# Turns, additions, scaling and row writes of a routing stage in another order

## The chip, the cores and the metric

The kernel runs on one core of one Trainium2 chip. The metric is device time in microseconds (us), median of three runs. Inputs and results are float32.

## The reference, cut to what matters

Two transformer blocks on 512 tokens of width 1024. The change lies in the first one, between the output projection of its second attention (`w_mo`) and its mixture of experts:

```
x = x + (memory attention output) @ w_mo            # 512 x 1024
h = rms_norm(x, norm_moe_w)
g = h @ w_group      (4 groups);  e = h @ w_router  (4 x 8 experts)
grp = argmax(g); top 2 experts of that group
gates = softmax(g)[grp] * softmax(top two logits)
for each expert: y = (silu(xb @ w_gate) * (xb @ w_up)) @ w_down   # xb = its rows of h
x = x + sum of gate * y
```

Every expert's three matrices of 2 MB are read: 32 x 3 x 2 MB.

## The kernel before, in words

Each engine has its own hand-written program, and the engines meet in counted semaphores: `X.tick(key)` raises one, `wait_ge(*X.at(key))` waits for it. An engine works strictly in the order in which its code was written.

The tokens are four tiles of 128 rows, i = 0 to 3. `w_mo` is two panels of 512 columns. `projecting` (L498) multiplies a panel in eight steps (half of the contraction, tile) of 12 matmuls of 128x512. The last panel uses the order `BY_TILE` (L494): (0,0) (0,1) (1,0) (1,1) (0,2) (1,2) (0,3) (1,3); I number these steps 0 to 7. A tile of the panel is done at its step with half 1: tile 0 after step 2, tile 1 after step 3, tile 2 after step 5, tile 3 after step 7. `behind[n]` is called after step n, `after(i)` when tile i is done.

`dve_router` (L1744) first splits the two weight units of the last panel (`dve_cut`, L451, behind `act_cut`, L440, on ScalarE; the second of them needs the buffer that panel 0 reads until its last matmul), then adds panel 0 to X (four `dve_add`, L1334), then handles the last panel tile by tile: add, mean of squares (ScalarE squares, L581; GpSimd takes the root, L591), copy of the turned features from PSUM, and `dve_scale` (L597), which writes the normed rows that go to memory as `scratch_h`.

`flip` turns (transposes) the 1024 columns of a tile of X in two halves of four 128x128 blocks: half 0 needs only panel 0's result, half 1 the last panel's. VectorE copies half 0 to SBUF, ScalarE half 1 (L1736). `logit(i)` multiplies tile i's turned features with the 36 router columns (8 float32 matmuls, recorded as 16). Before, flip(i) stands one tile late in the last panel and logit(i) two tiles late; flip(3), logit(2), logit(3) stand behind it.

PSUM has eight banks. `Banks.take` (L119) goes round among the banks of a set and makes TensorE wait until the last user of the bank has let it go. Followed through the code, panel 0 of `w_mo` has banks 0, 1, 2, 3 for tiles 0 to 3 and the last panel 4, 5, 0, 1. The turns use the set `LOGITS` = banks 2, 3, 7 in this order, the first of them bank 2, which is let go by the addition of panel 0's tile 2.

Behind the logits VectorE chooses the experts, TensorE counts how many tokens of each expert stand ahead (`count`), VectorE makes places of it, TensorE and VectorE turn these to lists of rows (`places`, `dve_rows`, L1828). GpSimd's program (`pool_router`, L1852, then L2106) waits until all four tiles of rows are written to `scratch_h` and the lists are there, and gathers the rows of the first expert pair by an indirect DMA. VectorE cleans the gathered rows (`dve_clean`, L1847: rows that stand for no token become zero), TensorE turns them, and the first product (L1962) starts. The gates (L1817 to L1824) stand behind this cleaning and are used behind the first product.

SyncE's queue: `sp_load` (L1923) loads one expert matrix (2 MB) to one of nine slots; loads 0 to 8 need no earlier load's slot. From load 9 on, a load waits until the product that read its slot's last content is done; loads 9 to 12 go in two parts, the first waits until half of the product is done. Before, loads 5 and 6 stand behind the end of the last panel and behind the row writes of tiles 0 to 2, load 7 behind that of tile 3, load 8 behind the landing of the first gather.

Of the kernel before, what the change touches and what calls it, by code (L numbers as in the profile page):

```python
# [13 lines left out]
ACT = mybir.ActivationFunctionType  # L14
# [5 lines left out]
NT = 4  # L20
# [419 lines left out]
def act_cut(k, u, part=None):  # L440

    w = k.w
    at = half_of(part, w.units[u][0] * w.units[u][1])
    k.A.wait_ge(*w.landed[u % RAW].at(u))
    if w.prior[u] is not None:
        k.A.wait_ge(*w.freed[w.prior[u]])
    k.A.e.activation(w.splits[w.split_of[u]][0][:, at], w.rows(u)[:, at], ACT.Copy).then_inc(  # L447
        *(w.half_hi if part == 0 else w.hi).tick(u))
# [30 lines left out]
def flips(k, bank, srcs):  # L479
    for n, s in enumerate(srcs):  # L480
        m = s.shape[0]
        ins = k.T.e.transpose(bank[0:s.shape[1], 128 * n:128 * n + m], s, k.ident[0:m, 0:m])  # L482
    return ins


def blocks_of(rows, n=8):
    return [rows[:, 128 * c:128 * c + 128] for c in range(n)]
# [50 lines left out]
def finish(steps):  # L538
    for _ in steps:
        pass  # L540
# [44 lines left out]
def dve_mean(k, site, i):  # L585
    ss = k.rstat[site, i]
    k.V.wait_ge(*k.squared.at(site, i))
    k.V.e.tensor_scalar(ss, ss, 1.0 / D, 1e-6, ALU.mult, ALU.add).then_inc(*k.meant.tick(site, i))
# [8 lines left out]
def dve_scale(k, site, i, src, rows, gain):  # L597
    k.V.wait_ge(*k.rooted.at(site, i))
    k.V.e.scalar_tensor_tensor(out=rows, in0=src, scalar=k.rstat[site, i], in1=gain, op0=ALU.mult,
                               op1=ALU.mult).then_inc(*k.rowed.tick(site, i))  # L600
# [733 lines left out]
def dve_add(k, name, half, i, scale):  # L1334

    V, ve = k.V, k.V.e
    xs, bank = k.X[:, i, 512 * half:512 * half + 512], k.banks[name, half, i]
    V.wait_ge(*k.projected.at(name, half, i))
    if scale is None:
        ins = ve.tensor_tensor(xs, xs, bank[:], ALU.add)  # L1340
    else:
        ins = ve.scalar_tensor_tensor(out=xs, in0=xs, scalar=scale, in1=bank[:], op0=ALU.mult, op1=ALU.add)
    ins.then_inc(*k.res.tick(name, half, i))
    V.wait_ge(*k.res.at(name, half, i))
# [104 lines left out]
def mem_out(k, half, **kw):  # L1449
    return projecting(k, "w_mo", half, k.start["w_mo"] + 2 * half, NT,  # L1450
                      lambda i: [k.mix_lo.at("mem", i, 0), k.mix_lo.at("mem", i, 1)],
                      lambda i: k.res.at("w_mo", half, i), **kw)
# [220 lines left out]
def pe_router(k):  # L1673
    T, te, u0 = k.T, k.T.e, k.start["w_mo"]
    logits = k.banks.take(T, ("logits",), k.dve_step.at("router", "logits"), hold=True, of=Banks.FLIPS)

    def flip(i):
        T.wait_ge(*k.res.at("w_mo", 1, i))
        for half in range(2):
            bank = k.banks.take(T, ("moe", i, half), (k.h_odd if half else k.h_even).at(i), of=Banks.LOGITS)  # L1680
            flips(k, bank, blocks_of(k.X[:, i, :])[4 * half:4 * half + 4]).then_inc(*k.h_turned.tick(i, half))

    def logit(i):
        T.wait_ge(*k.dve_step.at("router", "gain"))
        T.wait_ge(*k.h_even.at(i))
        T.wait_ge(*k.h_odd.at(i))
        group(te, logits[:, 36 * i:36 * i + 36],
              [(k.xn[:, c, 128 * i:128 * i + 128], k.rw[:, c, :]) for c in range(KT)]).then_inc(*k.pe_step.tick("router", i))

    def behind(i):  # L1690
        if i:
            flip(i - 1)
        if i > 1:
            logit(i - 2)
    finish(mem_out(k, 1, after=behind, steps=BY_TILE))
    flip(3)
    logit(2)
    logit(3)
    k.banks.release(("logits",))
    bank = k.banks.take(T, ("count",), k.dve_step.at("places", "marked"))  # L1700
    T.wait_ge(*k.dve_step.at("router", "chosen"))
    ones, strict = k.tri[:, 511:639], k.tri[:, 383:511]
    te.matmul(bank[:, 0:128], strict, k.ms, start=True, stop=True, skip_group_check=True)
    for c in (3, 2, 1):
        ins = te.matmul(bank[:, 128 - 32 * c:128], ones, k.ms[:, 0:c, :], start=False, stop=True, skip_group_check=True)
    ins.then_inc(*k.pe_step.tick("count"))
    bank = k.banks.take(T, ("total",), k.dve_step.at("router", "count"))
    ins = group(te, bank[:, 0:32], [(ones, k.ms[:, i, :]) for i in range(NT)])
    ins.then_inc(*k.pe_step.tick("total"))
    pe_places(k, "places", 0, NPAIR, k.pe_step, k.dve_step)  # L1710
# [15 lines left out]
def act_router(k):  # L1726
    A, ae, u0 = k.A, k.A.e, k.start["w_mo"]
    act_cut(k, u0 + 2)
    act_cut(k, u0 + 3)
    for i in range(NT):  # L1730
        A.wait_ge(*k.res.at("w_mo", 1, i))
        if i == 3:
            A.wait_ge(*k.hd_out[0].at())
        act_square(k, "moe", i, k.X[:, i, :], k.xg[i % 3])
        A.wait_ge(*k.h_turned.at(i, 1))
        ae.activation(k.xn[:, 4:8, 128 * i:128 * i + 128], k.banks["moe", i, 1][:].rearrange("p (k t) -> p k t", k=4),  # L1736
                      ACT.Copy).then_inc(*k.h_odd.tick(i))
    A.wait_ge(*k.dve_step.at("router", "less"))
    ae.activation(k.s44, k.s44, ACT.Exp).then_inc(*k.act_step.tick("router", "group"))
    A.wait_ge(*k.dve_step.at("router", "apart"))  # L1740
    ae.activation(k.dr[:, 0:4], k.dr[:, 0:4], ACT.Exp).then_inc(*k.act_step.tick("router", "pair"))


def dve_router(k):  # L1744
    V, ve, u0 = k.V, k.V.e, k.start["w_mo"]
# [6 lines left out]
    ve.tensor_tensor(k.rw, k.rw, k.gainT.unsqueeze(2).to_broadcast([P, 8, 36]), ALU.mult).then_inc(  # L1752
        *k.dve_step.tick("router", "gain"))
    V.wait_ge(*k.om_in[1].at("moe"))
    for i in range(NT):
        dve_add(k, "w_mo", 1, i, None)
        dve_mean(k, "moe", i)
        V.wait_ge(*k.h_turned.at(i, 0))
        ve.tensor_copy(k.xn[:, 0:4, 128 * i:128 * i + 128],
                       k.banks["moe", i, 0][:].rearrange("p (k t) -> p k t", k=4)).then_inc(*k.h_even.tick(i))  # L1760
        dve_scale(k, "moe", i, k.X[:, i, :], k.xg[i % 3], k.om[1][:])
    V.wait_ge(*k.pe_step.at("router", 3))
    b3 = k.banks["logits",][:, 0:144].rearrange("p (i n) -> p i n", i=4)
    rstd = k.rstd.unsqueeze(2)
# [32 lines left out]
    ve.tensor_tensor(dr[:, 0:4], k.em[:, :, 1], k.em[:, :, 0], ALU.subtract).then_inc(*k.dve_step.tick("router", "apart"))  # L1797
    m01 = k.m01.rearrange("p c i n -> p (c i) n")
    ve.tensor_tensor(k.token1[:, :, 0, :], m01, k.tokv.unsqueeze(2).to_broadcast([P, 8, 32]), ALU.mult)
    V.wait_ge(*k.pe_step.at("count"))  # L1800
    pos = k.banks["count",][:, 0:128].rearrange("p (i n) -> p i n", i=4)
    for c in range(2):
# [4 lines left out]
                     k.pk.unsqueeze(2).to_broadcast([P, 8, 64]), ALU.is_equal).then_inc(*k.dve_step.tick("places", "marked"))  # L1807
    V.wait_ge(*k.pe_step.at("places"))
    dve_rows(k, "places", NPAIR, k.dve_step)
    dve_clean(k, k.x1, 0)  # L1810
    V.wait_ge(*k.pe_step.at("total"))
    ve.tensor_copy(k.cnt, k.banks["total",][:, 0:32]).then_inc(*k.dve_step.tick("router", "count"))
    V.wait_ge(*k.dve_step.at("router", "count"))
# [9 lines left out]
    V.settle(ve.tensor_tensor(gate[:, 1, :], gate[:, 0, :], dr[:, 0:4], ALU.mult))  # L1823
    ve.tensor_tensor(k.token1[:, :, 1, :], m01, gate.rearrange("p c i -> p (c i)").unsqueeze(2).to_broadcast([P, 8, 32]),  # L1824
                     ALU.mult).then_inc(*k.dve_step.tick("gates", "marked"))


def dve_rows(k, what, n, dve_step):  # L1828
# [18 lines left out]
def dve_clean(k, x, n):  # L1847
    k.V.wait_ge(*x.gathered[n % 3].at(n))
    k.V.e.tensor_scalar(k.xg[n % 3], k.xg[n % 3], k.taken[:, n:n + 1], None, ALU.mult).then_inc(*x.cleaned.tick(n))
# [9 lines left out]
def sp_router(k):  # L1859
    Y, a, x, mo = k.Y, k.a, k.x1, k.start["w_mo"]  # L1860
    Y.wait_ge(*k.w.freed[mo - 1])
    sp_load(k, x, 0)
    Y.wait_ge(*k.w.lo.at(mo + 1))
    sp_load(k, x, 1)
    Y.wait_ge(*k.applied.at("mem", 15))
    Y.e.dma_start(k.rw[:, :, 0:4], a["w_group"][0].rearrange("(k p) n -> p k n", p=P)).then_inc(*k.c3_in.tick(0))
    for g in range(4):
        Y.e.dma_start(k.rw[:, :, 4 + 8 * g:12 + 8 * g],
                      a["w_router"][0, g].rearrange("(k p) n -> p k n", p=P)).then_inc(*k.c3_in.tick(1 + g))
    for n, (dst, src) in enumerate(((k.tri, a["c_tri"]), (k.iota, a["c_iota"]), (k.tokv, a["c_tok"]),  # L1870
                                    (k.gainT, a["l_moe"]), (k.cap, a["c_cap"]))):
        Y.e.dma_start(dst, src).then_inc(*k.c3_in.tick(5 + n))
    sp_load(k, x, 2)
    sp_load(k, x, 3)
    Y.wait_ge(*k.w.lo.at(mo + 3))
    sp_load(k, x, 4)
    for i in range(NT):
        if i == 3:
            Y.wait_ge(*k.projected.at("w_mo", 1, 3))
            sp_load(k, x, 5)  # L1880
            sp_load(k, x, 6)
        Y.wait_ge(*k.rowed.at("moe", i))
        Y.e.dma_start(k.hd[128 * i:128 * i + 128, :], k.xg[i % 3]).then_inc(*k.hd_out[i].tick())
    sp_load(k, x, 7)
    Y.wait_ge(*x.gathered[0].at(0))
    sp_load(k, x, 8)

# [1559 lines left out]
```

## Time and profile before

| | |
|---|---|
| median of three runs | 2345.57 us (2345.16 to 2345.81) |
| the profiled execution's own time | 2346.38 us |
| its span | 2345.1 us |
| TensorE busy | 2227.9 us, 95% |
| VectorE busy | 1020.5 us, 44% |
| ScalarE busy | 716.6 us, 31% |
| DMA | 370.27 MB, mean 158 GB/s |
| chain that ended last | TensorE 76%, DMA 9%, VectorE 6%, issue 5%, ScalarE 3% |

The busy shares are means over stages. The expert stage (about 510 to 990 us) has DMAs busy in all slices and the rest of the kernel does not, so the stage and not the mean tells what bounds it. PE is TensorE's matmuls, DVE VectorE, ACT ScalarE, POOL GpSimd, SPq SyncE's DMA issues.

### The profile page before, as it was taken

Reading aid. Unit: us, or ns where it says so; the run is one execution under the profiler, and the core shown is the slowest. Engines: PE = TensorE matmul, PEld = TensorE weight load, DVE = VectorE, ACT = ScalarE, POOL = GpSimd, SP = SyncE. Lnnn points to the kernel's source line nnn. Section 1 sums busy time; section 2 is a strip of 40 time slices with the busy share of each in tenths; the row PEclk is TensorE's granted clock in tenths of the full one; section 3 lists DMA queues with packets and bytes.
Section 4 is the critical chain, followed back from the end, with each engine's and each line's share of the span. In section 5 each row is a group of like instructions: output and inputs, shape, how many; then the busy total and the mean of one; then the engine's idle time right before and its main releaser. Section 6 shows DMA issues by size and latency. Waiting matters only on the chain.

```text
span 2345.1 us, 28330 instructions
## 1 busy us (share of the span) xinstructions
PE 2227.9 (95%) x11771; PEld 1642.0 (70%) x11771; DVE 1020.5 (44%) x1860; ACT 716.6 (31%) x1251; POOL 104.3 (4%) x109
## 2 busy tenths in 40 slices
PE   8998999979999899899879999999999999999998
PEld 7866787754433334488656788888878778888887
DVE  5356464332322222533567643233532456433334
ACT  5335354210100000222456233133233462331330
POOL 2001001010000000000000000000000001000001
PEclk9999999979999999999989999999999999999999
DMA  5233341369999999722110333222142202322320
GB/s 203 90 126 99 111 167 67 124 242 421 427 426 427 427 426 428 280 92 77 45 43 1 101 116 108 90 94 104 38 156 90 72 2 69 112 90 93 105 90 36
DMA packets 107316, 370.27 MB, mean 158 GB/s; under 512 B 15232, under 2 KB 20736, under 8 KB 94384
## 3 DMA queue, kind: packets, MB, share of 16 engines
q1 hardware_dynamic: 104160, 361.58, 40.6%
q0 software_dynamic: 3024, 6.83, 0.9%
q8 instruction: 95, 1.56, 0.3%
q14 instruction: 37, 0.30, 0.0%
HBM read 368.32 MB, written 4.19 MB: 159 GB/s over the span
## 4 chain that ended last, share of the span: by engine, by line
PE 76%; DMA 9%; DVE 6%; issue 5%; ACT 3%; POOL 1%; SPq 0%; DVEq 0%; ACTq 0%; POOLq 0%
PE PB L465 51%; PE PB L1962 10%; PE PB L482 4%; PE PB L784 4%; DMA FL_raw<-in_w_exp_gate 3%; PE PB L475 3%; PE PB L676 2%; DMA Z<-in_w_exp_gate 1%; DMA FH_raw<-in_w_exp_gate 1%; DMA W_raw<-in_w_exp_down 1%; PE PB L800 1%; DMA FL_raw<-in_w_exp_down 1%; PE PB L681 1%; ACT nsp L710 1%; DMA scratch_h<-Z 1%
## 5 line engine op out<-in xcount | busy, mean ns | idle before, releaser
L465 PE MATMUL PB<-W,FH 128*128 128x512 f32 (+1 forms) x1792 | 555.0, 392 | 8.0 <-DVE FL L845 4.0
L456 DVE TENSOR_TENSOR W<-R,W 128x2048 fp32r<-128x2048 f32 (+2 forms) x130 | 291.6, 2244 | 598.7 <-ACT W L447 598.7
L447 ACT ACTIVATE W<-R 128x2048 fp32r<-128x2048 f32 (+2 forms) x130 | 243.8, 1876 | 639.9 <-PE PB L465 636.2
L465 PEld LDWEIGHTS PB<-W,FH 128*128 128x128 f32 x1792 | 330.0, 189 | 76.0 <-issue 5.4
L465 PE MATMUL PB<-W,hid 128*128 128x512 f32 x1536 | 349.4, 390 | 0.0
L465 PE MATMUL PB<-W,FL 128*128 128x512 f32 (+1 forms) x896 | 347.5, 388 | 0.0
L465 PEld LDWEIGHTS PB<-W,hid 128*128 128x128 f32 x1536 | 288.3, 188 | 59.6
L465 PE MATMUL PB<-FH,W 128*128 128x512 f32 (+1 forms) x1152 | 324.2, 366 | 1.3 <-DVE FL L570 1.3
L465 PEld LDWEIGHTS PB<-FH,W 128*128 128x128 f32 x1152 | 208.5, 189 | 37.2 <-issue 1.8
L465 PE MATMUL PB<-FL,W 128*128 128x512 f32 (+1 forms) x576 | 210.7, 366 | 0.0
L465 PEld LDWEIGHTS PB<-W,FL 128*128 128x128 f32 x896 | 168.7, 188 | 34.5
L1962 PE MATMUL PB<-R,om 128*64 128x512 f32 x320 | 150.1, 625 | 15.2 <-DMA Z<-in_w_exp_gate 7.6
L1962 PE MATMUL PB<-Z,om 128*64 128x512 f32 x304 | 126.0, 616 | 0.8 <-issue 0.8
L465 PEld LDWEIGHTS PB<-FL,W 128*128 128x128 f32 x576 | 108.7, 189 | 17.5
L482 PEld LDWEIGHTS PB<-ident,nsp 128*128 128x128 f32 x674 | 80.1, 148 | 42.0 <-issue 27.2
L482 PE MATMUL PB<-ident,nsp 128*128 128x128 f32 x674 | 103.2, 282 | 5.3 <-ACT nsp L710 2.2
L710 ACT ACTIVATE nsp<-nsp,stat 128x512 f32<-128x512 f32 (+3 forms) x146 | 83.3, 572 | 74.9 <-DVE stat L692 74.5
L2037 ACT ACTIVATE tmp_r<-PB 128x512 fp32r<-128x512 f32 x32 | 17.4, 594 | 261.0 <-PE PB L1962 261.0
L676 PE MATMUL PB<-Z 64*128 64x512 f32 (+4 forms) x416 | 94.4, 517 | 2.7 <-ACT om L2735 1.8
L784 PE MATMUL PB<-ptr,Z 128*64 128x128 f32 (+1 forms) x768 | 78.9, 282 | 17.5 <-ACT ptr L734 10.8
L692 DVE CUSTOM_DVE_ANT_0 nsp<-PB,Z 128x512 f32<-128x512 f32 (+3 forms) x146 | 69.0, 510 | 53.0 <-PE PB L676 38.6
L1962 PEld LDWEIGHTS PB<-R,om 128*64 128x64 f32 x320 | 44.6, 144 | 65.2 <-issue 65.2
(340 smaller groups left out, 2576.5 us busy)
## 6 DMA issues: line engine op xcount, KB each, us to landing
R<-in_mlp_w_up SPq DMA_DIRECT2D x32, 1024.0 KB, 5.3
R<-in_mlp_w_down SPq DMA_DIRECT2D x32, 1024.0 KB, 4.9
Z<-in_w_exp_down SPq DMA_DIRECT2D x13, 2048.0 KB, 29.1
Z<-in_w_exp_up SPq DMA_DIRECT2D x12, 2048.0 KB, 34.2
R<-in_w_exp_gate SPq DMA_DIRECT2D x10, 2048.0 KB, 33.3
W_raw<-in_w_exp_up SPq DMA_DIRECT2D x10, 2048.0 KB, 31.3
R<-in_w_exp_up SPq DMA_DIRECT2D x9, 2048.0 KB, 30.9
R<-in_w_in SPq DMA_DIRECT2D x12, 1024.0 KB, 5.5
```

Source lines behind the costliest of these rows:

```text
L447: k.A.e.activation(w.splits[w.split_of[u]][0][:, at], w.rows(u)[:, at], ACT.Copy).then_inc(*(w.half_hi if part == 0 else w.hi).tick(u))
L456: k.V.e.tensor_tensor(wl[:, at], w.rows(u)[:, at], wh[:, at].bitcast(F32), ALU.subtract).then_inc(*(w.half_lo if part == 0 else w.lo).tick(u))
L465: ins = te.matmul(bank, l, r, start=(start and n == 0), stop=(stop and n == len(terms) - 1), skip_group_check=True)
L475: ins = te.matmul(bank, l, r, start=(n == 0), stop=(n == len(pairs) - 1))
L482: ins = k.T.e.transpose(bank[0:s.shape[1], 128 * n:128 * n + m], s, k.ident[0:m, 0:m])
L676: ins = k.T.e.matmul(bank[:, 0:t.n], t.q, t.keys, start=True, stop=(t.more is None))
L681: k.T.e.matmul(bank[:, 0:t.n], *t.more, start=False, stop=True).then_inc(*k.scored.tick(*t.key))
L692: V.e.tensor_tensor_reduce(ns[:, 0:t.n], k.banks[("scores",) + t.key][:, 0:t.n], t.tab, 1.0, FAR, ALU.add, ALU.min, peak(k, m)).then_inc(* ...
L710: k.A.e.activation(ns[:, 0:t.n], ns[:, 0:t.n], ACT.Exp, bias=peak(k, m), scale=-1.0, accum_out=t.den).then_inc(*k.exped.tick(*t.key))
L784: ins = T.e.matmul(k.banks["sums", *t.bank[0]][t.rows, at], l, r, start=first, stop=last, skip_group_check=True)
L800: ins = T.e.matmul(bank[rows, 128 * c:128 * c + 128], col, k.ident[:], start=True, stop=True, skip_group_check=True)
L1962: ins = T.e.matmul(bank[64 * side:64 * side + 64, :], lhs[:, 128 * c + 64 * side:128 * c + 64 * side + 64], ws[side][:, c, at], start=(c = ...
```

## The change

Five edits. (1) Turns are made by halves and earlier: behind step 0 turn (tile 0, half 0), behind step 1 (1,0), step 3 (0,1), step 4 (1,1) and (2,0), step 5 logit(0), step 6 (2,1), (3,0) and logit(1); behind the panel logit(2), turn (3,1), logit(3). VectorE copies tile 3's second half too, which ScalarE did. (2) VectorE's order is written out: the last tile's addition stands ahead of its mean and its copy, with the earlier tiles' scaling moved between. (3) The scaling of tile 3 stands behind the choice, ahead of the wait for `count`. (4) The row writes move from SyncE's to ScalarE's queue; that of tile 3 stands behind both exponentials. Loads 5, 6 and 7 stand directly behind the end of the last panel. (5) The gates stand ahead of the first cleaning.

```diff
--- before.py
+++ after.py
@@ -1674,11 +1674,10 @@
     T, te, u0 = k.T, k.T.e, k.start["w_mo"]
     logits = k.banks.take(T, ("logits",), k.dve_step.at("router", "logits"), hold=True, of=Banks.FLIPS)
 
-    def flip(i):
-        T.wait_ge(*k.res.at("w_mo", 1, i))
-        for half in range(2):
-            bank = k.banks.take(T, ("moe", i, half), (k.h_odd if half else k.h_even).at(i), of=Banks.LOGITS)
-            flips(k, bank, blocks_of(k.X[:, i, :])[4 * half:4 * half + 4]).then_inc(*k.h_turned.tick(i, half))
+    def flip(i, half):
+        T.wait_ge(*k.res.at("w_mo", half, i))
+        bank = k.banks.take(T, ("moe", i, half), (k.h_odd if half else k.h_even).at(i), of=Banks.LOGITS)
+        flips(k, bank, blocks_of(k.X[:, i, :])[4 * half:4 * half + 4]).then_inc(*k.h_turned.tick(i, half))
 
     def logit(i):
         T.wait_ge(*k.dve_step.at("router", "gain"))
@@ -1687,14 +1686,18 @@
         group(te, logits[:, 36 * i:36 * i + 36],
               [(k.xn[:, c, 128 * i:128 * i + 128], k.rw[:, c, :]) for c in range(KT)]).then_inc(*k.pe_step.tick("router", i))
 
-    def behind(i):
-        if i:
-            flip(i - 1)
-        if i > 1:
-            logit(i - 2)
-    finish(mem_out(k, 1, after=behind, steps=BY_TILE))
-    flip(3)
+    def middle():
+        flip(1, 1)
+        flip(2, 0)
+
+    def late():
+        flip(2, 1)
+        flip(3, 0)
+        logit(1)
+    finish(mem_out(k, 1, steps=BY_TILE, behind={0: lambda: flip(0, 0), 1: lambda: flip(1, 0), 3: lambda: flip(0, 1),
+                                                4: middle, 5: lambda: logit(0), 6: late}))
     logit(2)
+    flip(3, 1)
     logit(3)
     k.banks.release(("logits",))
     bank = k.banks.take(T, ("count",), k.dve_step.at("places", "marked"))
@@ -1727,18 +1730,27 @@
     A, ae, u0 = k.A, k.A.e, k.start["w_mo"]
     act_cut(k, u0 + 2)
     act_cut(k, u0 + 3)
+
+    def store(i):
+        A.wait_ge(*k.rowed.at("moe", i))
+        ae.dma_start(k.hd[128 * i:128 * i + 128, :], k.xg[i % 3]).then_inc(*k.hd_out[i].tick())
     for i in range(NT):
         A.wait_ge(*k.res.at("w_mo", 1, i))
         if i == 3:
+            store(2)
             A.wait_ge(*k.hd_out[0].at())
         act_square(k, "moe", i, k.X[:, i, :], k.xg[i % 3])
-        A.wait_ge(*k.h_turned.at(i, 1))
-        ae.activation(k.xn[:, 4:8, 128 * i:128 * i + 128], k.banks["moe", i, 1][:].rearrange("p (k t) -> p k t", k=4),
-                      ACT.Copy).then_inc(*k.h_odd.tick(i))
+        if i < 3:
+            A.wait_ge(*k.h_turned.at(i, 1))
+            ae.activation(k.xn[:, 4:8, 128 * i:128 * i + 128], k.banks["moe", i, 1][:].rearrange("p (k t) -> p k t", k=4),
+                          ACT.Copy).then_inc(*k.h_odd.tick(i))
+        if i in (1, 2):
+            store(i - 1)
     A.wait_ge(*k.dve_step.at("router", "less"))
     ae.activation(k.s44, k.s44, ACT.Exp).then_inc(*k.act_step.tick("router", "group"))
     A.wait_ge(*k.dve_step.at("router", "apart"))
     ae.activation(k.dr[:, 0:4], k.dr[:, 0:4], ACT.Exp).then_inc(*k.act_step.tick("router", "pair"))
+    store(3)
 
 
 def dve_router(k):
@@ -1752,13 +1764,32 @@
     ve.tensor_tensor(k.rw, k.rw, k.gainT.unsqueeze(2).to_broadcast([P, 8, 36]), ALU.mult).then_inc(
         *k.dve_step.tick("router", "gain"))
     V.wait_ge(*k.om_in[1].at("moe"))
-    for i in range(NT):
-        dve_add(k, "w_mo", 1, i, None)
-        dve_mean(k, "moe", i)
-        V.wait_ge(*k.h_turned.at(i, 0))
-        ve.tensor_copy(k.xn[:, 0:4, 128 * i:128 * i + 128],
-                       k.banks["moe", i, 0][:].rearrange("p (k t) -> p k t", k=4)).then_inc(*k.h_even.tick(i))
+
+    def features(i, half):
+        V.wait_ge(*k.h_turned.at(i, half))
+        ve.tensor_copy(k.xn[:, 4 * half:4 * half + 4, 128 * i:128 * i + 128],
+                       k.banks["moe", i, half][:].rearrange("p (k t) -> p k t", k=4)).then_inc(
+            *(k.h_odd if half else k.h_even).tick(i))
+
+    def scale(i):
         dve_scale(k, "moe", i, k.X[:, i, :], k.xg[i % 3], k.om[1][:])
+    features(0, 0)
+    features(1, 0)
+    dve_add(k, "w_mo", 1, 0, None)
+    dve_mean(k, "moe", 0)
+    dve_add(k, "w_mo", 1, 1, None)
+    scale(0)
+    dve_mean(k, "moe", 1)
+    scale(1)
+    features(2, 0)
+    dve_add(k, "w_mo", 1, 2, None)
+    dve_mean(k, "moe", 2)
+    features(3, 0)
+    scale(2)
+    dve_add(k, "w_mo", 1, 3, None)
+    features(3, 1)
+    dve_mean(k, "moe", 3)
+    V.wait_ge(*k.rooted.at("moe", 3))
     V.wait_ge(*k.pe_step.at("router", 3))
     b3 = k.banks["logits",][:, 0:144].rearrange("p (i n) -> p i n", i=4)
     rstd = k.rstd.unsqueeze(2)
@@ -1797,6 +1828,7 @@
     ve.tensor_tensor(dr[:, 0:4], k.em[:, :, 1], k.em[:, :, 0], ALU.subtract).then_inc(*k.dve_step.tick("router", "apart"))
     m01 = k.m01.rearrange("p c i n -> p (c i) n")
     ve.tensor_tensor(k.token1[:, :, 0, :], m01, k.tokv.unsqueeze(2).to_broadcast([P, 8, 32]), ALU.mult)
+    scale(3)
     V.wait_ge(*k.pe_step.at("count"))
     pos = k.banks["count",][:, 0:128].rearrange("p (i n) -> p i n", i=4)
     for c in range(2):
@@ -1807,7 +1839,6 @@
                      k.pk.unsqueeze(2).to_broadcast([P, 8, 64]), ALU.is_equal).then_inc(*k.dve_step.tick("places", "marked"))
     V.wait_ge(*k.pe_step.at("places"))
     dve_rows(k, "places", NPAIR, k.dve_step)
-    dve_clean(k, k.x1, 0)
     V.wait_ge(*k.pe_step.at("total"))
     ve.tensor_copy(k.cnt, k.banks["total",][:, 0:32]).then_inc(*k.dve_step.tick("router", "count"))
     V.wait_ge(*k.dve_step.at("router", "count"))
@@ -1823,6 +1854,7 @@
     V.settle(ve.tensor_tensor(gate[:, 1, :], gate[:, 0, :], dr[:, 0:4], ALU.mult))
     ve.tensor_tensor(k.token1[:, :, 1, :], m01, gate.rearrange("p c i -> p (c i)").unsqueeze(2).to_broadcast([P, 8, 32]),
                      ALU.mult).then_inc(*k.dve_step.tick("gates", "marked"))
+    dve_clean(k, k.x1, 0)
 
 
 def dve_rows(k, what, n, dve_step):
@@ -1874,14 +1906,9 @@
     sp_load(k, x, 3)
     Y.wait_ge(*k.w.lo.at(mo + 3))
     sp_load(k, x, 4)
-    for i in range(NT):
-        if i == 3:
-            Y.wait_ge(*k.projected.at("w_mo", 1, 3))
-            sp_load(k, x, 5)
-            sp_load(k, x, 6)
-        Y.wait_ge(*k.rowed.at("moe", i))
-        Y.e.dma_start(k.hd[128 * i:128 * i + 128, :], k.xg[i % 3]).then_inc(*k.hd_out[i].tick())
-    sp_load(k, x, 7)
+    Y.wait_ge(*k.projected.at("w_mo", 1, 3))
+    for u in range(5, 8):
+        sp_load(k, x, u)
     Y.wait_ge(*x.gathered[0].at(0))
     sp_load(k, x, 8)
```

## Rows read from the trace of the kernel before

**Rows 1.** The page's 40 slices: DMA share in tenths.

```profile
DMA  5233341369999999722110333222142202322320
```

**Rows 2.** Stretches of the span: busy times, then granted clock, DMA share, GB/s.

```profile
522.00:523.00 1.00, 1.00 (x6) 0.35 (x4) 0.00 (x0) 0.00 (x0) 0.00 (x0) 0.64 0.08 33
...
524.35:600.00 75.65, 74.59 (x390) 31.87 (x387) 21.26 (x34) 8.10 (x15) 3.96 (x4) 1.00 1.00 416
...
900.00:956.00 56.00, 50.47 (x236) 21.66 (x232) 16.28 (x26) 4.84 (x9) 0.16 (x1) 1.00 1.01 428
```

**Rows 3.** The chain that ended last, 474 to 956 us: start, duration, what.

```profile
474.69 5.47 PE PB L465 x24
480.17 0.87 PE PB L482 x8
481.04 1.71 PE PB L475 x16
...
494.67 13.76 DMA scratch_h<-Z
...
509.45 4.47 DMA Z<-scratch_h,Z
...
515.17 1.97 PE PB L482 x8
...
517.97 9.42 PE PB L1962 x32
...
933.79 22.15 DMA FL_raw<-in_w_exp_down
```

**Rows 4.** VectorE in order of time, 467 to 518 us: start, duration, line, what.

```profile
467.19 2.85 DVE L1340 TENSOR_TENSOR X<-X,PB 128x512 f32<-128x512 f32 x4
...
488.77 0.69 DVE L1759 COPY FH_raw<-PB 128x512 f32<-128x512 f32 x1 [4.20 <-PE PB L482]
...
493.35 1.29 DVE L599 SCALAR_TENSOR_TENSOR Z<-X,stat,om 128x1024 f32<-128x1024 f32 x1
496.26 0.17 DVE L1765 TENSOR_TENSOR Z<-PB,stat 128x16 f32<-128x16 f32 x1 [1.62 <-PE PB L475]
...
501.31 0.42 DVE L1799 TENSOR_TENSOR nsp<-Z 128x256 f32<-128x256 f32 x1
503.25 0.49 DVE L1803 TENSOR_TENSOR tmp<-PB,Z 128x128 f32<-128x128 f32 x2 [1.51 <-PE PB L1705]
...
507.12 0.17 DVE L1834 TENSOR_TENSOR Z<-tmp,Z 128x16 uint32<-128x16 f32 x1
...
516.76 0.43 DVE L1824 TENSOR_TENSOR nsp<-Z 128x256 f32<-128x256 f32 x1
```

**Rows 5.** ScalarE, TensorE and SyncE's queue in order of time.

```profile
463.03 1.92 ACT L447 ACTIVATE W<-R 128x2048 fp32r<-128x2048 f32 x1 [3.52 <-PE PB L465]
...
491.30 1.09 PE L482 MATMUL PB<-ident,X 128*128 128x128 f32 x8 [0.43 <-DVE X L1340]
...
491.04 0.43 SPq L1940 DMA_DIRECT2D FL_raw<-in_w_exp_gate  x1
...
523.97 0.33 SPq L1940 DMA_DIRECT2D Z<-in_w_exp_down  x1
```

**Rows 6.** Stretches with a falling or rising granted clock, columns as in Rows 2.

```profile
495.00:496.00 1.00, 1.00 (x8) 1.00 (x7) 0.00 (x0) 0.00 (x0) 0.00 (x0) 0.70 0.87 360
...
663.00:664.00 1.00, 0.76 (x4) 0.00 (x0) 0.00 (x0) 0.17 (x1) 0.00 (x0) 1.00 1.04 442
...
666.00:667.00 1.00, 0.39 (x2) 0.32 (x4) 1.00 (x2) 0.00 (x0) 0.00 (x0) 0.54 1.00 426
...
669.00:670.00 1.00, 1.00 (x6) 0.42 (x4) 0.00 (x0) 0.00 (x0) 0.00 (x0) 0.76 0.92 393
```

**Rows 7.** DMA issues, whole span: count, KB each, median us from issue to landing.

```profile
scratch_h<-Z SPq DMA_DIRECT2D x4, 512.0 KB, 2.8
Z<-scratch_h,Z POOLq DMA_INDIRECT x16, 10.4
```

## The prediction

> **What bounds the kernel now.** I read first the page's slices [rows 1]: the DMAs are busy without a gap from the tenth slice to the sixteenth, while the kernel as a whole uses 158 GB/s. Then the stretches of that part [rows 2]: from 524 us on the 16 DMA engines have share 1.00 and 416 GB/s, at the end 1.01 and 428 GB/s; just before, at 522 to 523, the share is 0.08. The chain [rows 3] ends its weight stage on such a transfer (started 933.79, landed 955.94) and not on arithmetic. So from load 9 on, issued at 523.97 [rows 5], when half of the first expert product is done, the stage is a fixed quantity of bytes: loads 9 to 95 are 87 x 2.097 MB = 182.5 MB, which in 432 us (523.97 to 955.94) is 422 GB/s, with the gathers 427 to 428. Nothing behind 524 can be made up or lost there: **each us by which the first product starts earlier or later goes to the end one to one.** The question is thus what the change does to the 60 us ahead of it.
>
> There the chain runs, in order [rows 3]: the last panel with its turns and logits, tile 3's row write (issued 494.67, landed 13.76 us later, at 508.43), the first gather (from 509.45, 4.47 us), cleaning and turning, the first product at 517.97. Beside it runs a second chain, VectorE's [rows 4]: logits at 496.26, choice, places, the lists of rows ready at 507.29 (507.12 plus 0.17). It is 1.1 us shorter than the row write's. A change has to shorten both to win more than 1.1 us, and lengthening the second by more than 1.1 us already costs.
>
> **Edit 1, the turns.** The turn behind step 0 waits for two things: panel 0's addition of tile 0, and bank 2, which that panel's tile 2 holds. VectorE makes the four additions from 467.19 in 2.85 us [rows 4], 0.71 each, so the third ends at 469.3. They can't come earlier: they stand behind VectorE's cut, that needs ScalarE's (463.03 to 464.95), and that waited for TensorE to end panel 0 [rows 5]. TensorE itself: steps 4 and 5 begin at 474.69 behind the turn of tile 0 (0.87), so step 3 ends at 473.82; a step takes 5.47 / 2 = 2.735 us [rows 3], so step 0 began at 473.82 - 4 x 2.735 = 462.9 and ends at 465.6. Before, no turn was due until 473.8 and no wait showed. After, TensorE stands in its order at a turn that can't start: 469.35 - 465.6 = **+3.7 us** on the engine that both chains need. Nothing hides it: steps 1 to 7 are queued behind.
>
> *Clock.* Idle TensorE of this length is not in this stretch of the trace. The nearest: idle from 663.76, back at 666.6; the granted clock fell to half at about 666.1 (mean 0.54) and was back at 669.5 (mean 0.76) [rows 6], 3.4 us at half. Work in half clock loses half its time, so bounds are 0 and 1.7 us. If it falls 2.3 us into the idle time and stays 3.4, it lasts to 471.3 and meets 2.0 us of work: **+1.0**.
>
> *Tail.* The work is the same in number: eight steps, eight half turns of 0.435 (0.87 per pair), four logits of 1.71 [rows 3]. The idle 0.43 ahead of turn 3 [rows 5] goes, since logit(2) now covers the addition: **-0.4**. But turn (3,1), its copy and logit(3) now follow each other with nothing between: 0.69 for the copy [rows 4], some 0.2 for two hand-overs and the end of the turn: **+0.9** (bounds 0.7 and 1.2). At 495 to 496 the clock was falling (0.70) [rows 6]; from 495.4 to 496.2 the last logit ran at half. With the dense steps ending later it is likely spared: **-0.4** (to 0). Other turns wait for nothing: their halves and banks are free by over 1 us in the order written out. Sum to the logits: 3.7 + 1.0 - 0.4 + 0.9 - 0.4 = **+4.8** (3.8 to 6.2): 501.1 in place of 496.26.
>
> **Edits 2 and 3, VectorE.** The last addition still follows step 7 directly; mean, root and scalings lie under TensorE's work. The scaling of tile 3, 1.29 us, comes behind the instruction at 501.31 and ahead of the one at 503.25, which waits 1.51 us for `count` [rows 4]: 501.7 to 502.95, 0 us. Without that cover (a `count` at full clock, some 0.9 us shorter) it would cost what `count` gains. So the lists come at 507.29 + 4.8 = **512.1** (511.1 to 513.5).
>
> **Edit 4, the row writes.** Tile 3's rows were ready at 494.64; now behind the choice: 501.73 + 4.8 + 1.29 = 507.8, issued at 508.0. The three weight loads used to be issued from 491.04 [rows 5] among the row writes; now at the end of step 7: 462.9 + 8 x 2.735 + 7 x 0.435 + 2 x 1.71 + 4.7 = 495.9. Their 6.29 MB take 14.7 us at 427 GB/s and 1 us to start, to 511.7. Where the row write lands beside them is not in the trace. Alone it takes 2.8 (the median of four, three on a quiet DMA) [rows 7]: 510.8. Behind everything: 511.7 + 2.8 = 514.5. Nearest row: gathers, from GpSimd's queue, land in a median of 10.4 us [rows 7] beside queued loads, and in 4.47 on quiet DMAs [rows 3], so a second queue gets a small share while loads are queued. I take 513.0. For tiles 0 to 2 nothing changes.
>
> In sentences that the sum does without: the Trainium skill (DMA: Bandwidth & Descriptors, section Queues, rings and completion order) says that every DMA engine goes round between the queues that have work, a packet at a time; by it the write would take half the bandwidth at once and land at about 511.9, before the lists. The same page (Issuing engines are not separate DMA queues) says that another issuing engine saves only the time to issue, which would put it near 513.5. The gathers' 10.4 us lean to the second.
>
> GpSimd then wakes at max(512.1, 513.0) = 513.0 in place of 508.43: **+4.6** (2.7 to 7.1). Its 1.0 us to the gather and the gather's 4.47 stay.
>
> **Edit 5, gates.** They ended at 517.19 [rows 4], 0.05 behind the turns of the first rows (515.17 plus 1.97 us [rows 3]), whose copy waited on both: less than 0.1 us is won. In their new place they lie between the lists and the landing, 5 us with VectorE idle: 0.
>
> **First product.** Its first 4.7 us ran at half clock (517.97 to 522.7, mean 0.64 at 522 to 523) [rows 2], 2.4 us lost. Where the clock comes back after a start that is later by another amount, no row says; bounds 0 and -2.4; nearest is its own row, so **-0.3**.
>
> Sum: 4.6 - 0.3 = +4.3. Against the profiled execution's 2346.38 that is 2350.7; that execution lies 0.8 above the median of the runs, so for the median 2345.57 + 4.3 = **2349.9 us**, +0.18%. I count 0.2% (4.7 us) as what can be told from no change, so this is "same", close to the edge. Its own range is 2347.6 to 2351.0.
>
> **Rivals.**
> *A, the row write waits out the loads.* Place: tile 3's write on ScalarE's queue. Landing at 514.5, with a clock loss nearer 1.7 at 515.1: GpSimd wakes 6.1 to 6.7 later, the end is 5.8 to 6.4 later: 2351.6, slower. It decides from a landing behind 513.1. For it: the same write took 13.76 us among loads before; the 10.4 of the gathers. Against it: only some 3 us of load are left when it starts.
> *B, the lists decide.* The write shares evenly with the loads (the skill's first rule above) and lands before 512.1: 512.1 - 508.43 = 3.7, less 0.3: 2349.0. For it: 0.5 MB is little; against it: the gathers.
> *C, the change does what it says.* TensorE is not held at the turn of step 0, because the additions or the bank come earlier than I read. Then the choice is at 496.3 or 0.1 to 0.4 later, lists at 507.5, row write covered: -1.0, with up to 2.4 from the clock: 2344.5 (2342.2 to 2345). For it: the tail wait of 0.43 goes, the write's 13.76 us leave the chain. Against it: the cut and the additions keep their order in the code and end at 469.3 in the trace.
>
> **How the numbers follow.** Forecast 0.42, A 0.36, B 0.13, C 0.09. "Same" takes six sevenths of the forecast, B, and about two thirds of C: 0.36 + 0.13 + 0.06 = 0.55. Slower is A and the rest of the forecast: 0.42 less a part in which A's landing is met by an early clock: 0.40. Faster 0.05, from C at its low end and what I don't see. The range leaves out the lowest part of C and the upper tail of A (every bound at its worst is +6.8): 2346.6 to 2352.2.
>
> **What would show it.** TensorE idle of 3.7 us from 465.6, ended by VectorE's additions; a stretch at half clock behind it; the last logit at about 501; the lists at 512; tile 3's write issued at 508; the gather at 514; load 9 at about 528; the stage's DMA share 1.0 to about 960. No idle at 465 makes step 1 wrong; a landing before the lists makes B right; an end of the weight stage that moves less than load 9 makes the one to one wrong.

## The result, and the profile of the changed kernel

The changed kernel takes 2353.01 us (median of 7 runs, 2352.15 to 2356.05) against 2345.57 (7 runs, 2341.34 to 2349.18): ratio 1.0036, 95% interval 1.0027 to 1.0045. It is slower by 7.4 us, more than the 4.3 that I forecast (2349.9), and outside my range (2346.6 to 2352.2).

The profiled execution took 2352.52 us, span 2350.4. First its chain, against [rows 3]:

```profile
470.06 0.70 DVE X L1340
...
470.89 1.08 PE PB L482 x4
471.98 3.60 PE PB L465 x12
...
498.25 1.71 PE PB L475 x16
499.96 0.48 PE PB L482 x4
...
500.54 0.70 DVE FH_raw L1770
...
501.37 1.96 PE PB L475 x16
...
510.13 10.32 DMA scratch_h<-Z
...
521.46 3.54 DMA Z<-scratch_h,Z
...
528.63 8.56 PE PB L1989 x32
```

TensorE waits for VectorE's third addition, makes the half turn of tile 0 in 1.08 us where one takes 0.44, and needs 3.60 for a step of 2.735: the granted clock is at half (1.2 GHz) until 473.6. At the end the copy (L1770) stands alone between a turn and the last logit. Then tile 3's row write takes 10.32 us and the gather follows.

VectorE, against [rows 4], and the idle TensorE ahead of its first turn:

```profile
503.43 0.17 DVE L1796 TENSOR_TENSOR Z<-PB,stat 128x16 f32<-128x16 f32 x1 [2.14 <-PE PB L475]
...
508.48 0.42 DVE L1830 TENSOR_TENSOR nsp<-Z 128x256 f32<-128x256 f32 x1
508.81 1.28 DVE L599 SCALAR_TENSOR_TENSOR Z<-X,stat,om 128x1024 f32<-128x1024 f32 x1
510.41 0.49 DVE L1835 TENSOR_TENSOR tmp<-PB,Z 128x128 f32<-128x128 f32 x2 [0.32 <-PE PB L1708]
...
514.29 0.17 DVE L1866 TENSOR_TENSOR Z<-tmp,Z 128x16 uint32<-128x16 f32 x1
```

```profile
470.89 1.08 PE L482 MATMUL PB<-ident,X 128*128 128x128 f32 x4 [3.81 <-DVE X L1340]
...
501.37 1.95 PE L475 MATMUL PB<-tmp,FH_raw 128*128 128x36 f32 x16 [0.94 <-DVE FH_raw L1770]
```

The scaling (L599) lies in the wait for `count`, of which 0.32 us is left: it is free, as forecast. The lists are ready at 514.46.

All times of this execution are 1.44 us late from its first weight cut on (9.18 us for 7.74, a wait for a DMA), long before the change, so I count from the end of panel 0, which each trace shows by ScalarE's second cut ([rows 5]: 463.03, less 0.14 us; in the changed kernel 464.47). In that count:

| us from the end of panel 0 | before | changed | moved |
|---|---|---|---|
| loads 5 to 7 from | 28.15 | 33.96 | +5.8 |
| logits on VectorE | 33.37 | 39.10 | +5.7 |
| lists ready | 44.40 | 50.13 | +5.7 |
| tile 3's write issued | 31.78 | 45.80 | +14.0 |
| it lands | 45.54 | 56.11 | +10.6 |
| first gather issued | 46.56 | 57.13 | +10.6 |
| load 9 issued | 61.08 | 69.45 | +8.4 |
| next stage's first weight cut on ScalarE | 505.46 | 515.54 | +10.1 |

The span is only 5.3 us longer though the stage lost 10. Matched by ScalarE's instructions, the two executions are 11.5 us apart (1.44 of it from the start) at 968 us of the one before, 8.7 at 1130 and 5.4 at 1201. In between the granted clock differs: of the stretches at half clock that begin between 960 and 1230 us the execution before has six and this one four. That is this pair of executions; the runs of one kernel spread over up to 12 us, and the medians differ by 7.4.

### The profile page after: what moved, and what is told of

Its sections match the earlier page's. It is cut to its first block, busy times and chain, and to the rows that moved or that the text cites. A ratio compares the mean times of both kernels' runs of the same rounds, so it can differ in the third digit from the quotient of the medians.

```text
span 2350.4 us, 28333 instructions
## 1 busy us (share of the span) xinstructions
PE 2223.9 (95%) x11771; PEld 1638.5 (70%) x11771; DVE 1021.4 (43%) x1861; ACT 716.0 (30%) x1250; POOL 104.2 (4%) x109
## 4 chain that ended last, share of the span: by engine, by line
PE 76%; DMA 9%; DVE 6%; issue 5%; ACT 3%; POOL 1%; SPq 0%; DVEq 0%; ACTq 0%; POOLq 0%
PE PB L465 51%; PE PB L1989 9%; PE PB L482 4%; PE PB L784 4%; DMA Z<-in_w_exp_gate 3%; PE PB L475 3%; DMA FH_raw<-in_w_exp_gate 3%; PE PB L676 2%; DMA Z<-in_w_exp_down 1%; DMA FL_raw<-in_w_exp_gate 1%; PE PB L800 1%; PE PB L681 1%; ACT nsp L710 1%; DMA scratch_h<-Z 0%; DVE X L2286 0%
## 5 line engine op out<-in xcount | busy, mean ns | idle before, releaser
L1989 PEld LDWEIGHTS PB<-R,om 128*64 128x64 f32 x320 | 44.6, 144 | 65.7 <-issue 65.7
```

The source lines that it names most:

```text
L1989: ins = T.e.matmul(bank[64 * side:64 * side + 64, :], lhs[:, 128 * c + 64 * side:128 * c + 64 * side + 64], ws[side][:, c, at], start=(c = ...
```

## The experiments

Times vary with the clock, so I judge by the count from panel 0's end and put the time beside it; a ratio is that to the kernel before. Each count is from one profiled execution. How far it repeats is seen at the logits: 33.1 to 33.5 in the five kernels whose code is the same up to there as before (before, experiments 5, 9, 10 and 11), but 39.0 to 41.1 in the six with the stalled turns (changed, 2, 3, 6, 7 and 8), by the granted clock.

**1. No turn behind steps 0 and 1.**

```diff
-behind={0: lambda: flip(0, 0), 1: lambda: flip(1, 0), 3: ...
+behind={2: first, 3: ...          # first: flip(0, 0), flip(1, 0)
```

> The changed kernel with one edit taken back in part: the turns of tiles 0 and 1, half 0, stand behind step 2 of the last panel and not behind steps 0 and 1. Theory (stall): TensorE doesn't stand idle for 3.8 us ahead of them and the clock doesn't fall behind it, so from the end of panel 0 to the logits it takes 5.3 us less (about 33.7 in place of 39.0), and the end of the last panel, the weight loads 5 to 7, the lists and the row write of tile 3 all come earlier by the same, the first gather and load 9 too: time 5 us below the changed kernel, 2 to 3 above the kernel before. Rival (the row write alone is the loss, and it waits for the loads whatever comes before): the logits come 5 us earlier but the time of the gather is set by a write that takes longer than 10.3 us, time within 1.5 us of the changed kernel.

Logits at 34.80 (4.3 us earlier than changed), load 9 at 64.30 (5.2 earlier); 2348.47 us, ratio to before 1.0010 (0.9999 to 1.0021). The idle time and its clock are gone; the last logit took 2.98 us, mostly at half clock, for 1.96, which is the missing us. The write now took 8.54, 1.8 less. The stall theory holds: 5.2 of the 8.4 us at load 9 go with the idle time, the write behind it moving along and growing shorter.

**2. The write without loads beside it.**

```diff
-    for u in range(5, 8): sp_load(k, x, u)
-    Y.wait_ge(*x.gathered[0].at(0)); sp_load(k, x, 8)
+    sp_load(k, x, 5)
+    Y.wait_ge(*x.gathered[0].at(0))
+    for u in range(6, 9): sp_load(k, x, u)
```

> The changed kernel with weight loads 6 and 7 held back until the first gather has landed, where they stood ahead of the row write of tile 3. Theory (the write waits behind the queued loads): tile 3's rows, issued at the same place, land 2.6 to 3.5 us after issue and not 10.3, the gather starts 6 us earlier relative to the end of panel 0, limited by the lists; load 9 is then issued about 6 us earlier, but 4.2 MB more are still to move behind the gather, 9.8 us of DMA, so the time is 0 to 5 us above the changed kernel. Rival (a write issued by ScalarE is slow by itself): it still takes about 10 us.

Tile 3's write, issued at the same 45.84, landed 2.61 us later and no longer ends the wait: the lists (50.17) do (L1843 is VectorE's instruction right behind them), and the gather is issued at 51.11, 6.0 us earlier than in the changed kernel. Tile 2's write, beside load 5 alone, still took 9.33. The median landing of all four writes is 2.7 us:

```profile
517.01 1.13 POOL L2133 DMA_INDIRECT Z<-scratch_h,Z  x1 [13.48 <-DVE Z L1843]
```

```profile
scratch_h<-Z ACTq DMA_DIRECT2D x4, 512.0 KB, 2.7
```

In the changed kernel the median of the four is 6.5. Time 2356.3 us, ratio 1.0039 (1.0025 to 1.0053): load 9 comes at 64.81, but the bytes held back are then missing (450 us from load 9 to the next stage, elsewhere 444 to 447). ScalarE's queue is not slow by itself; the loads beside it are the cause. This answers the rival.

**3. Scaling and write of tile 3 early.**

```diff
-    V.wait_ge(*k.rooted.at("moe", 3))
+    scale(3)                                  # and not behind token1; store(3) ahead of both Exp
```

> The changed kernel with edit 3 taken back: tile 3 is scaled ahead of the choice and its row write stands ahead of the exponentials, issued about 7.5 us earlier. Theory (the write lands when the loads queued at the end of the panel are through, about 19 to 20 us after these were issued): it lands at most 2 to 3 us earlier than in the changed kernel, still behind the lists or together with them; the logits' evaluation starts up to 1 us later since the scaling of 1.29 us stands ahead of it where it isn't covered; time 1 to 4 us below the changed kernel. Rival (the write takes a fixed 10.3 us from issue): it lands 7.5 us earlier, ahead of the lists, which then decide: 5 us below.

The write was issued at 39.21 and took 13.52 us, landing at 52.73, behind the lists (51.99); load 9 at 66.32; 2351.72 us, ratio 1.0025 (1.0012 to 1.0037). Issued 6.6 us earlier, it lands 3.4 us earlier: not a fixed time from issue. It had tile 2's write ahead of it in its queue, which landed at 46.62. In this execution the last logit ran at half clock, so the logits came at 40.96; the early scaling did not hold them up (VectorE still waited 1.77 us for them).

**4. Edit 4 alone on the kernel before.** All four writes from ScalarE's queue, loads 5 to 7 directly behind the panel.

```diff
+        if i in (1, 2): store(i - 1)          # in act_router; store(2) at i == 3, store(3) behind the loop
-        Y.wait_ge(*k.rowed.at("moe", i)); Y.e.dma_start(k.hd[...], k.xg[i % 3])
```

> The kernel before with edit 4 alone: row writes from ScalarE's queue, that of tile 3 directly behind its scaling, loads 5 to 7 directly behind the end of the last panel. Theory: loads 5 to 7 are issued 2.7 to 6 us earlier than before, so the DMAs are through about 3 us earlier, and tile 3's write, issued at 494.7 as before, lands by then, 505 to 506; the lists at 507.3 decide and the first gather starts about 1 us earlier: time 0 to 1.5 us below the kernel before. Rival (a write from ScalarE's queue gets less than from SyncE's): it lands later than 508.4, time 1 to 4 us above the kernel before.

A miss for my theory: loads from 25.43 on, write issued at 32.15 and 16.84 us long, landing at 48.99, 3.5 us later than before, as the rival had it; load 9 at 62.92, 1.8 later. 2346.51 us, ratio 1.0002 (0.9992 to 1.0012), so the time doesn't show it. Three writes stood in ScalarE's queue beside the loads at once and landed one after the other, at 38.5, 44.6 and 49.0:

```profile
490.97 2.40 ACTq L1733 DMA_DIRECT2D scratch_h<-Z  x2
496.80 0.33 ACTq L1733 DMA_DIRECT2D scratch_h<-Z  x1
```

How queues share the DMAs is seen in the changed kernel's packets: queue, packets, MB, share of 16 engines, for 496 to 520 us and then for 510.1 to 513.8, 513.8 to 517.2 and 517.2 to 520.4:

```profile
q1 hardware_dynamic: 432, 6.29, 65.4%
q10 hardware_dynamic: 288, 1.05, 10.8%
...
q1 hardware_dynamic: 107, 1.49, 95.1%
q10 hardware_dynamic: 11, 0.04, 2.7%
...
q1 hardware_dynamic: 76, 1.05, 74.2%
q10 hardware_dynamic: 89, 0.36, 26.0%
...
q10 hardware_dynamic: 46, 0.12, 9.6%
q1 hardware_dynamic: 7, 0.05, 3.7%
```

q1 is SyncE's queue, q10 ScalarE's. 6.29 MB in 432 packets less 48 of 4 bytes is 16 KB each; two writes (tiles 2 and 3) in 288 less 32 are 4 KB each. Until 513.6, 3.5 us behind its issue, tile 3's write moves nothing; then a 4 KB packet goes about one to one with a 16 KB packet (89 to 76), a quarter of the bytes. The DMAs are through with nearly all at 518; until 520 a trickle runs on at share 0.07 and 0.06, that is one DMA engine of 16. In experiment 5, where no other write is in that queue, the counts for 498.9 to 505 us are cleaner (0.52 MB is a quarter of 2.08, so one 4 KB packet for each of 16 KB):

```profile
q1 hardware_dynamic: 143, 2.08, 79.7%
q10 hardware_dynamic: 142, 0.52, 21.0%
```

The Trainium skill (DMA: Bandwidth & Descriptors, section Queues, rings and completion order) has the turns by packets, and these counts agree with it; that turns are not shares of bandwidth is what I overlooked. What becomes of unequal packets this section does not say; these traces show it.

**5. Only tile 3's write on ScalarE's queue.** The kernel before; tiles 0 to 2 stay with SyncE, loads 5 to 7 together behind them.

```diff
+    A.wait_ge(*k.rowed.at("moe", 3))          # in act_router, ahead of the first Exp
+    ae.dma_start(k.hd[384:512, :], k.xg[0]).then_inc(*k.hd_out[3].tick())
```

> The kernel before with only the row write of tile 3 moved to ScalarE's queue, issued at the same place; tiles 0 to 2 stay in SyncE's queue, so nothing stands ahead of it in its own. Theory (queues take turns by packets, 4 KB of the write against 16 KB of a load; 8 packets a DMA engine, so 8 x 0.73 us plus some 3 us to the first): it lands about 10 us after its issue, at 41 to 43 us from the end of panel 0 in place of 45.5, ahead of the lists (44.4), which then decide: gather 1.1 us earlier than before, time 0 to 2 us below the kernel before. Rival (the write lands only when the loads issued ahead of it are through): as before, 13 to 14 us, no gain.

```profile
scratch_h<-Z ACTq DMA_DIRECT2D x1, 512.0 KB, 10.7
```

Issued at 31.78, landed at 42.5, ahead of the lists (44.23), which decide; gather at 45.17, load 9 at 58.59, 2.5 earlier than before. With three loads ahead in the other queue it took 10.7 us, where behind two loads in SyncE's own queue it had taken 13.76: so a queue of its own gains it 3 us here. 2340.1 us, ratio 0.9979 (0.9969 to 0.9990).

**6. Tile 3's write in SyncE's queue, behind the loads.** The changed kernel with `store(3)` moved behind `sp_load` 7.

> The changed kernel with tile 3's row write in SyncE's queue, behind loads 5 to 7, with its issue where the scaling ends as in the change. Theory (turns by packets): behind the 3 loads it is served last but then at the full rate, so it lands about when the queue is empty, 54 to 55.5 us from the end of panel 0 against 56.1: 0 to 2 us earlier than in the changed kernel. Rival (ScalarE's queue is fast, the loads only slow it a little): it lands later than in the changed kernel.

A miss: 9.43 us, landing at 57.15. In this execution the logits were at 41.03, 1.9 us late, which moves all of it: the half clock behind TensorE's idle time lasted 6.8 us and not 3.4. So the landing is later than in the changed kernel, as the rival said, but for this reason: counted from the loads' issue it is 21.7 us, in the changed kernel 22.15. 2354.87 us, ratio 1.0041 (1.0025 to 1.0057). So at this place either queue gives nearly the same: the write ends with the loads.

**7. Loads 5 to 7 in packets of 8 KB.**

```diff
+        for part in range(2): sp_load(k, x, u, part)
```

> The changed kernel with loads 5, 6 and 7 each issued in two parts, which makes their packets 8 KB in place of 16 KB; bytes and order are the same. Theory (turns by packets): each 4 KB packet of the row write now waits for 8 KB, about 0.3 us, so tile 3's write takes 8 x 0.45 us plus up to 3 us, 6 to 8 us in place of 10.3, and the gather comes 2.5 to 4 us earlier. Rival (bandwidth is shared in halves, or the write waits for all loads ahead): it lands within 1 us of where it did, since the bytes ahead of it are the same.

```profile
512.30 8.12 DMA scratch_h<-Z
```

Landing 2.2 us sooner after issue, 8.12 against 10.32, just outside the 6 to 8 that I expected; the logits of this execution were 2.0 us late too, so the gather gained 0.2 and not 2.5 to 4. Time 2353.24, ratio 1.0033 (1.0022 to 1.0044). By itself the landing proves nothing, since the loads had 0.8 us more of a lead (12.65 us against 11.84). The packets of 516 to 518.5 us say more: 80 against 93, still about one for one, though a load's packet is now 8 KB, and the write gets 31% of the bytes and not a quarter:

```profile
q1 hardware_dynamic: 93, 0.74, 69.6%
q10 hardware_dynamic: 80, 0.33, 31.8%
```

**8. The turns without edits 3 and 4.**

> The changed kernel with edits 3 and 4 taken back: scaling of tile 3 ahead of the choice, row writes and loads 5 to 7 in SyncE's queue as before. What is left is the order of the turns, of VectorE and of the gates. Theory (the turns cost 5.3 to 7 us by TensorE's idle time and clock, the late and slow write some 2 to 3 more): logits at 39 to 41 us from the end of panel 0, tile 3's write issued at about 39 behind loads 5 and 6 and landing 12 to 13 us later at 51.5, together with the lists at 50 to 52; load 9 at 66 to 67, 5 to 6 above the kernel before. Rival (the late write is the whole loss): load 9 within 2 us of the kernel before.

Logits at 39.02, lists at 50.05, write issued at 38.93 and landed ahead of the lists; gather at 50.98, load 9 at 64.99, 3.9 above before where I expected 5 to 6. 2351.07 us, ratio 1.0023 (1.0012 to 1.0033). The turns alone cost 3.9 of the 8.4 us, by a chain in which the write has no part; the other 4.5 come with edits 3 and 4, as the late write among the loads. The rival (within 2 us) falls.

**9. Gates alone** on the kernel before.

> The kernel before with edit 5 alone: the gates ahead of the first cleaning. Theory: the gates ended 0.05 us behind the turns that they ran beside, so 0 to 0.2 us is won between the landing of the first gather and the first product; time equal to the kernel before within what can be told. Rival (the gates held up the cleaning or the count's reader before): over 1 us below.

Load 9 at 60.89 (61.08); 2344.0 us, ratio 1.0004 (0.9993 to 1.0014): nothing, as forecast.

**10. Late scaling alone**, write in SyncE's queue between loads 6 and 7.

> The kernel before with edit 3 alone: tile 3 is scaled behind the choice; its row write stays in SyncE's queue, now issued at about 40 us from the end of panel 0 and not 31.8, with load 7 behind it. Theory (a write is late by what is queued ahead of it, not by its own size): loads 5 and 6, issued at 28.15, are nearly through at 41, so the write lands 3 to 5 us after its issue, at 43 to 45, about with the lists (44.2): the gather starts at 45 to 46 with load 7 beside it, which makes it 1 to 4 us longer; load 9 at 60 to 63, time within 2 us of the kernel before. Rival (a late scaling costs its delay of 8 us wherever it stands): the write lands at 53, load 9 at 69, time 8 us above.

```profile
504.85 0.33 SPq L1886 DMA_DIRECT2D scratch_h<-Z  x1
505.22 0.43 SPq L1943 DMA_DIRECT2D W_raw<-in_w_exp_up  x1
```

```profile
510.12 1.13 POOL L2109 DMA_INDIRECT Z<-scratch_h,Z  x1 [14.65 <-DVE Z L1837]
```

Issued at 39.80, 8 us later than before, it took 3.68 us and still landed ahead of the lists: GpSimd's wait is ended by VectorE (L1837, ready at 44.13), not by a DMA. Load 9 at 59.30; 2343.79 us, ratio 0.9998 (0.9987 to 1.0008). Lateness costs nothing here, where loads 5 and 6, issued 11.6 us earlier, are nearly through and no third load is queued ahead.

**11. Experiment 5 and the gates.**

> The kernel before with tile 3's row write alone on ScalarE's queue and loads 5 to 7 together (the version that was 5.8 us below the kernel before), and the gates ahead of the first cleaning. Theory: lists decide, gather at 45.2 us from the end of panel 0, load 9 at 58.5 to 60, time 3 to 6 us below the kernel before (2340 to 2343). Rival (that run's gain was chance of the clock): within 1.5 us of the kernel before.

Load 9 at 58.13, as expected, but 2343.73 us against 2344.43, ratio 0.9995 (0.9984 to 1.0005): a miss in time. The 5.8 us of experiment 5 are more than its stage gained (2.5 to 3 us in both traces), and did not come again with an edit that alone does nothing. The interval of this run (3.7 us faster to 1.2 slower) leaves room for the stage's 2.5 to 3 us and for nothing. I take these as shown by the traces, and the rest of the 5.8 as open.

**12. Turns mended, writes as in experiment 5.**

> The changed kernel's turns with the first two behind step 2 (no idle time), tile 3 scaled ahead of the choice, and the row writes as in the version that was 5.8 us below the kernel before. Theory (half turns and the copy between turn and last logit cost 1.4 us, scaling ahead of the evaluation up to 1.9 us more): logits at 34.8 to 36.7 us from the end of panel 0 against 33.2, write landed before the lists, gather at 46.8 to 48.7, load 9 at 60.5 to 62.5: 1.5 to 4 us above that version, within 2 us of the kernel before. Rival (turns by halves are good once the idle time is gone): logits at or below 33.2.

Logits at 34.39, gather at 46.37, load 9 at 58.74; 2345.24 us, ratio 1.0004 (0.9992 to 1.0016). Load 9 comes 1.8 us earlier than the earliest that I expected. The half turns put the logits 1.2 us behind those of experiment 5 (33.20) and bring nothing; the scaling ahead of the logits costs nothing (VectorE still waited 0.83 us for them). Experiment 1 has the same turns, but scales tile 3 late and writes all rows from ScalarE's queue; beside it load 9 is 5.6 us earlier. So with the stall mended the way in which the rows are written is still worth 5.6 us.

## Why the prediction was wrong

**The bound**, right. The stage from load 9 on is a quantity of bytes: from load 9 to the next stage's first cut it is 444.4 us before, 446.1 in the changed kernel, 444.5 to 446.8 in all the others but experiment 2, which held bytes back. One to one holds within 2.4 us.

**The turns**, right in mechanism and place. Idle 3.81 us (forecast 3.7). The clock cost 1.5 (0.64 in the turn, 0.87 in step 1) where I took 1.0 of at most 1.7. Wait ahead of the last logit 0.94 (0.9). With smaller terms the sum is 5.7 for 4.8, inside its bounds (their lower end adds up to 3.6, not 3.8, which changes nothing).

**Scaling and gates**, right: 0 each.

**The row write is the step that failed: "I take 513.0"**, that is 5.0 us from issue, bounds 2.8 to 6.5; it took 10.32. Less the 1.44 us, it was issued at 508.7 (I had 508.0) and landed at 519.0, so 6.0 us are missing here, and the whole change, +7.4, lies outside even my "every bound at its worst" of +6.8. Two terms of it were wrong. First the loads: I had them through 15.8 us from issue, at 427 GB/s. In the changed kernel the DMAs were still at share 0.96 at 516 to 517, 18 us behind the issue at 498.29, and a trickle ran on to 520:

```profile
516.00:517.00 1.00, 0.00 (x0) 0.00 (x0) 0.86 (x4) 0.00 (x0) 0.00 (x0) 0.50 0.96 389
...
518.00:519.00 1.00, 0.00 (x0) 0.00 (x0) 0.00 (x0) 0.00 (x0) 0.00 (x0) 0.50 0.07 29
519.00:520.00 1.00, 0.00 (x0) 0.00 (x0) 0.00 (x0) 0.00 (x0) 0.00 (x0) 0.50 0.06 25
```

"For tiles 0 to 2 nothing changes" was wrong: tile 2's write, issued at 490.68 before, ahead of the loads, now stands behind the end of the panel and is issued at 499.01, among them. I had left out its bytes, those of tile 3's own write, that the loads were issued 0.9 us later than I had them and moved only 229 and 262 GB/s in their first two us, and the trailing engine. The trace before could have warned me: there loads 5 to 7 and the writes of tiles 2 and 3, 7.29 MB, kept the DMAs busy from 491 to 510, 19 us. Second, I took it as landing 1.3 us behind the end of the loads, when none of its packets is served for 3.5 us, then each waits for one of theirs, and the slowest engine ends it. Rival A had the sign (slower) at 0.36 and nearly the mechanism, a write that ends only with the loads, though it doesn't wait behind them but runs among their last. Even its price, landing at 514.5 to 515.1, was too small: +10.6 at the gather, where it had 6.1 to 6.7. The range's upper end came from these bounds.

**What came back** (load 9 +8.4 for a gather +10.6): the gather took 3.54 us, not 4.47, on DMAs that were quiet by then; its cleaning began 0.4 us sooner behind its landing, for a reason that I did not look for; and the first product ran at half clock for 3 us, not 4.7, which is 0.85 us up to load 9. I had -0.3 for the clock. The forecast of the whole was 3.1 us too low and that of the stage's end 5.8; that the medians differ by 7.4 and not by the stage's 10.1 was not foreseen, and is not shown beyond the one pair of executions above.

**Rival C** is excluded by the idle time itself, **rival B** by the write's landing at 56.11, 6 us behind the lists; experiment 2 shows that with the loads away the lists do decide, at 50.17.

What stays open: which DMA engine trails and why, and how much of experiment 5's 5.8 us is more than chance.

## What to carry to other kernels

A turn or any small job put behind an earlier step must have its inputs by then, its PSUM bank included; on an engine that works in order, one early job that waited 3.8 us cost 5.3 with the clock, and the later ones only earn it back if something waited for them. A short transfer on which a chain hangs should be issued before bulk loads or with few of them left ahead in any queue: a queue of its own made it 3 us shorter (13.8 to 10.7) but did not free it (2.6 with no load beside it), and other short transfers in that queue stood ahead of it too. Price such a transfer from the moment when the same bulk traffic was really through in a trace, trailing engine included, and not from the mean rate.

## What the runs showed of the hardware

With loads running in SyncE's queue, the first 4 KB packet of tile 3's write in ScalarE's queue came 3.5 us behind its issue (3.6 in experiment 5), then about one for each 16 KB packet of a load. On quiet DMAs a write of 512 KB took 2.6 to 2.7 us. Beside loads, in ScalarE's queue, tile 3's took 8.1 to 10.7 us where no other write was still in front of it for more than 1.3 us, 13.5 with one in front and 16.8 with two; a write issued within 1 us of the loads or beside the first of them, with none in front, took 9.3 to 12.3. Idle TensorE of 3.8 us was followed by half clock for the next 2.7 us of work:

```profile
471.00:472.00 1.00, 1.00 (x5) 1.00 (x6) 0.89 (x3) 0.00 (x0) 0.00 (x0) 0.50 0.92 393
...
473.00:474.00 1.00, 1.00 (x4) 0.77 (x3) 0.00 (x0) 0.00 (x0) 0.00 (x0) 0.69 0.95 410
474.00:475.00 1.00, 1.00 (x6) 0.80 (x5) 0.00 (x0) 0.00 (x0) 0.00 (x0) 1.00 1.11 475
```
